# Index projection moved to the front of a hybrid RWKV/sparse-attention block, with the top-k search run beside the recurrence's preparation

## The reference, cut to what matters

```python
h = rms_norm(x, norm_mix_pre)
z = h @ w_in                      # 31 column blocks of 128
y_rwkv = rwkv7_time_mix(z_rwkv)   # r, zw, k, v, za, zg -> decays, normed keys, gates, then a scan
y_dsa  = dsa_attention(z_dsa)     # q, k, v, and index queries qi, index keys ki, index weights wi
x = x + rms_norm(concat(y_rwkv, y_dsa) @ w_out, norm_mix_post)
# then the feed-forward and the gated embedding, untouched
```

## Time and profile before

| what | value |
|---|---|
| median of 3 runs (lowest, highest) | 1964.87 us (1964.84, 1968.67) |
| the profiled execution | 1967.77 us |
| its span in the profile | 1966.3 us |
| mean granted TensorE clock | 0.947 |
| TensorE busy | 1714.4 us, 87% |
| VectorE busy | 1128.1 us, 57% |
| ScalarE busy | 771.0 us, 39% |
| GpSimd busy | 330.3 us, 17% |

### The profile page before, as it was taken

The page is one execution under the profiler, slowest core; times in us unless marked ns, Lnnn a source line. Parts: engine busy times, 40 slices in busy tenths (PEclk is TensorE's granted clock), DMA queues, the critical chain, the costliest instruction groups (busy, mean ns, idle before and its releaser), DMA issues. The chain is left out here.

```text
span 1966.3 us, 34355 instructions
## 1 busy us (share of the span) xinstructions
PE 1714.4 (87%) x14040; PEld 1388.2 (71%) x14040; DVE 1128.1 (57%) x2151; ACT 771.0 (39%) x1206; POOL 330.3 (17%) x299
## 2 busy tenths in 40 slices
PE   1899985599849995888759999999999999999996
PEld 0777663278727774777637888888888888888785
DVE  5267644779946652576643756544445654444755
ACT  4153432577535552333224433332233332322541
POOL 2232230031112210122311211000011000000422
PEclk9999997899959997999969999999999999999998
DMA  2115551122210005111035232233332333323222
GB/s 109 58 57 171 172 177 48 48 75 86 76 44 33 33 12 212 31 63 53 15 111 201 96 97 96 88 97 97 98 97 94 103 112 107 97 97 97 86 74 87
DMA packets 92182, 177.13 MB, mean 90 GB/s; under 512 B 7616, under 2 KB 51680, under 8 KB 92032
## 3 DMA queue, kind: packets, MB, share of 16 engines
q1 hardware_dynamic: 62336, 159.28, 24.4%
q10 hardware_dynamic: 29696, 15.73, 2.8%
HBM read 138.81 MB, written 36.18 MB: 89 GB/s over the span
## 5 line engine op out<-in xcount | busy, mean ns | idle before, releaser
L809 PE MATMUL acc<-h_hi,w_hi 128*128 128x512 f32 x768 | 304.8, 397 | 21.9 <-DVE w_lo L877 15.8
L810 PE MATMUL acc<-h_lo,w_hi 128*128 128x512 f32 x768 | 301.0, 392 | 0.0
L811 PE MATMUL acc<-h_hi,w_lo 128*128 128x512 f32 x768 | 300.9, 392 | 0.0
L713 ACT ACTIVATE w_hi<-w_raw 128x1024 fp32r<-128x1024 f32 x160 | 168.3, 1052 | 142.3 <-DMA w_raw<-w_ffn 142.0
L877 DVE TENSOR_TENSOR w_lo<-w_raw,w_hi 128x1024 fp32r<-128x1024 f32 x160 | 206.4, 1291 | 7.5 <-ACT w_hi L713 7.5
L809 PE MATMUL acc<-ffn_hi_lo,w_hi 128*128 128x512 f32 x512 | 200.3, 391 | 1.3 <-DVE ffn_hi_lo L925 1.3
L810 PE MATMUL acc<-ffn_hi_lo,w_hi 128*128 128x512 f32 x512 | 199.2, 389 | 0.0
L811 PE MATMUL acc<-ffn_hi_lo,w_lo 128*128 128x512 f32 x512 | 199.2, 389 | 0.0
L809 PEld LDWEIGHTS acc<-h_hi,w_hi 128*128 128x128 f32 x768 | 145.6, 190 | 55.1 <-DVE w_lo L877 16.6
L504 POOL TENSOR_TENSOR post_squares_total<-post_squares_total,post_squares 128x512 f32<-128x512 f32 x40 | 57.0, 1425 | 692.8 <-ACT post_squares L497 691.3
L810 PEld LDWEIGHTS acc<-h_lo,w_hi 128*128 128x128 f32 x768 | 145.5, 189 | 31.6 <-issue 1.7
(11 more groups left out here) (307 smaller groups left out, 3585.6 us busy)
## 6 DMA issues: line engine op xcount, KB each, us to landing
w_raw<-w_ffn SPq DMA_DIRECT2D x128, 512.0 KB, 3.4
rwkv_factors<-factors_then_masks ACTq DMA_DIRECT2D x28, 512.0 KB, 6.3
factors<-rwkv_factors SPq DMA_DIRECT2D x32, 448.0 KB, 6.8
w_in_first_raw<-w_in SPq DMA_DIRECT2D x19, 512.0 KB, 3.9
w_raw<-w_out SPq DMA_DIRECT2D x16, 512.0 KB, 3.6
w_raw<-w_gate SPq DMA_DIRECT2D x16, 512.0 KB, 3.4
w_in_raw<-w_in SPq DMA_DIRECT2D x12, 512.0 KB, 4.1
x_in<-xT SPq DMA_DIRECT2D x8, 512.0 KB, 6.7
```

What stands on the lines that cost most here:

```text
L713: act.activation(wh[:, g % RING, :], w_raw[:, g % RING, :], ACT.Copy).then_inc(rounded, 1)
L809: pe.matmul(out, w_hi, a_hi, start=first, stop=False)
L810: pe.matmul(out, w_hi, a_lo, start=False, stop=False)
L811: return pe.matmul(out, w_lo, a_hi, start=False, stop=last)
```

## The change

The norm of the input and the first five blocks become one stage, `project_index`, by halves of time: the first half of x is loaded, normed and multiplied while the second half is loaded and normed. The five blocks are the index key and weight block and the four index query blocks; their results stay on the chip. The layer norm of the index keys runs inside this stage. The mean of squares is now taken by TensorE per row block (no adding by VectorE), and all remainders of `h` are made by VectorE. `index_scores` follows at once and reads queries and keys in place. All other 26 blocks, the preparation of the recurrence and the search are one stage: 5 blocks first (low-rank, then the first pair's r, k, v), then three blocks per step for four pairs, then nine. SyncE now issues the seven stores of a pair's factors. The z blocks of r, k, v, the low-rank and the index blocks are no longer stored.

```diff
+ORDER = [KI_BLK] + [QI_BLK + b for b in range(PAIRS)] + list(range(QI_BLK)) + [b + p for b in (Q_BLK, AK_BLK, AV_BLK) for p in range(PAIRS)]
+def project_index(nc, io, common, gain, x, hi, lo, qz, kiT, wi, w):
+    units = [(0, 0), (1, 0), (0, 1), (1, 1)] + [(j, h) for j in range(2, INDEX_BLKS) for h in range(NH)]
+        def _(sp):
+            for h in range(NH):
+                for k in range(KB):
+                    sp.dma_start(x[:, k, cut[h]], io["xT"][:, k, cut[h]]).then_inc(x_loaded[h][k], 16)
+                    if h == 0 and k % 4 == 3:
+                        sp.dma_start(w.raw[:, k // 4, :], io["w_in"][ORDER[k // 4]]).then_inc(w.loaded[k // 4], 16)
+        def _(act):
+            for k in range(KB):
+                square(0, k)
+            nx[0].take_root(act)
+            w.start_rounding(act)
+            for k in range(3):
+                square(1, k)
+            for k in range(KB):
+                round_row(0, k)
+                if k + 3 < KB:
+                    square(1, k + 3)
...
+            for n in range(2, len(units)):
+                j, h = units[n]
+                copy(n)
+                if h == 1 and j + 2 < INDEX_BLKS + 2:
+                    w.round(act, j + 2, (j + 2) // 2, j % 2)
+        def _(pe):
+            for k in range(KB):
+                nx[0].sum(pe, k)
+            nx[0].spread_inverse(pe, 0)
+            for n, (j, h) in enumerate(units):
+                for k in range(KB):
+                    if n == 0:
+                        nx[1].sum(pe, k)
+                    if j == 0:
+                        pe.wait_ge(lo_ready, h * KB + k + 1)
...
+def project_and_select(nc, io, zT, hi, lo, out, rw, dec, score, mask, causal, room, va, near, vec, w):
+    BITS_AT = {WA: (0, 1, 2), G: (3, 4), FIRST_PAIR: (5, 6), FIRST_PAIR + 1: (7, 8), FIRST_PAIR + 2: (9, 10, 11)}
+    BITS_OF_PAIR = [(12, 13), (14, 15), (16, 17), (18, 19)]
+    BITS_AT.update({22: (20, 21, 22), 23: (23, 24, 25), 24: (26, 27, 28), 25: (29, 30, 31)})
+    BIAS_AT = 24
+        def _(sp):
+            for p in range(PAIRS):
...
+                sp.wait_ge(done, p + 1)
+                sp.wait_ge(vmixed, p + 1)
+                sp.wait_ge(gate_copied, p + 1)
+                for q in range(7):
+                    sp.dma_start(rw[p, :, :, q, :].rearrange("i f t -> f i t"), out[:, q, :].rearrange("f (i t) -> f i t", i=TILES)).then_inc(stored, 16)
+                load(b + 4)
+        def _(act):
+            for j in range(WA, HEAD):
+                if j > WA:
+                    round_weights(j + 1)
+                counts(BITS_AT[j])
+                copy(j)
+                if j == FIRST_PAIR + 1:
+                    act.activation(wa[0:N, :], out[0:N, 0, :], ACT.Tanh).then_inc(acted_wg, 1)
+                    act.activation(wa[N:P, :], out[N:P, 0, :], ACT.Copy).then_inc(acted_wg, 1)
+                    act.activation(sg[:, :], out[:, 1, :], ACT.Sigmoid).then_inc(acted_wg, 1)
+                    square_kk(0)
+            for p in range(PAIRS):
+                act.wait_ge(normed, p + 1)
+                act.activation(root[:, :], ps_k[:, :], ACT.Sqrt).then_inc(rooted, 1)
+                act.wait_ge(low_rank, p * 3 + 2)
+                act.activation(rate, ps_w[:, :], ACT.Sigmoid, bias=par[:, W0:W0 + 1]).then_inc(gates, 1)
+                act.activation(a, ps_a[:, :], ACT.Sigmoid, bias=par[:, A0:A0 + 1]).then_inc(gates, 1)
+                round_weights(b + 1)
+                act.wait_ge(summed, p * 2 + 2)
+...
+                copy(b)
+                round_weights(b + 2)
+                act.activation(out[:, GATE, :], ps_g[:, :], ACT.Copy).then_inc(gate_copied, 1)
+                counts(BITS_OF_PAIR[p])
+                copy(b + 1)
+                round_weights(b + 3)
+                if p + 1 < PAIRS:
+                    square_kk(p + 1)
+                copy(b + 2)
+            act.wait_ge(stored, PAIRS * STORED)
+            for j in range(FIRST_Q + 3, BLKS):
+                round_weights(j + 1)
+                counts(BITS_AT.get(j, ()))
+                copy(j)
+                if j == BIAS_AT:
+                    for h in range(HEADS):
+                        act.activation(vec[:, h, :], ps_b[:, h % 2, 0:BVEC], ACT.Copy).then_inc(bias_copied, 1)
+                if j > FIRST_V:
+                    copy_values(j - 1)
+            copy_values(BLKS - 1)
+            for j, t in enumerate(tiles):
+                act.wait_ge(selected, j + 1)
+                act.activation(mask[t][:, :], above[j % 2][:, 0:(t + 1) * P], ACT.Copy, scale=-NEG, bias=NEG).then_inc(mask_out, 1)
+        def _(pe):
+            for p in range(PAIRS):
+                pe.wait_ge(squares, p + 1)
+                by_half(ps_k, same_head[:, :], sq).then_inc(normed, 1)
+                by_half(ps_w, w2a2[0:N, :], wa[0:N, :]).then_inc(low_rank, 1)
+                pe.wait_ge(rooted, p + 1)
+                by_half(ps_a, w2a2[N:P, :], wa[N:P, :]).then_inc(low_rank, 1)
+                multiply(b)
+                by_half(ps_g, g2[:, :], sg).then_inc(low_rank, 1)
+                multiply(b + 1)
+                multiply(b + 2)
+            for j in range(FIRST_Q + 3, BLKS):
+                multiply(j)
+                if j == BIAS_AT:
+                    for h in range(HEADS):
+                        if h >= 2:
+                            pe.wait_ge(bias_copied, h - 1)
+                        pe.matmul(ps_b[:, h % 2, 0:BVEC], table[:, h, :], onehot, start=True, stop=True).then_inc(biased, 1)
+                if j > FIRST_V:
+                    turn_values(j - 1)
+            turn_values(BLKS - 1)
+        def _(dve):
+            for p in range(PAIRS):
+                dve.wait_ge(rooted, p + 1)
+                link(dve.tensor_scalar(root[:, :], root[:, :], 1e-12, None, ALU.max))
+                link(dve.reciprocal(inv[:, :], root[:, :]))
+                dve.wait_ge(gates, p * 2 + 2)
+                dve.tensor_tensor_scan(csum[:, :], keep[:, :], rate, 0.0, ALU.mult, ALU.add).then_inc(summed, 1)
...
+                dve.tensor_tensor(out[:, K_T, :], k, e_neg, ALU.mult).then_inc(done, 1)
+                find_bits(BITS_OF_PAIR[p])
+                if p + 1 < PAIRS:
+                    shift(p + 1)
...
+            for j, t in enumerate(tiles):
+...
+                if j >= 2:
+                    dve.wait_ge(mask_out, j - 1)
+                dve.scalar_tensor_tensor(above[j % 2][:, c], score[t][:, :], best[:, j:j + 1], eq[:, c], ALU.is_gt, ALU.add).then_inc(selected, 1)
```

More of the change, by code:

```diff
@@ L966, with square, sum, take_root @@
 A_T, R_T, B_T, K_T, V_T, BONUS, GATE = range(7)
-def project_and_prepare(nc, io, zT, hi, lo, out, rw, dec, w):
-    HEAD = PAIR_BLK + 3
-    COUNT = KI_BLK + 1
+class StreamedNorm(HalfNorm):
+    def square(self, act, k, src):
+        need(act, self.summed, k - self.ring + 1)
+        act.activation(self.sq[:, k % self.ring, :], src, ACT.Square).then_inc(self.squared, 1)
+    def sum(self, pe, k):
+        pe.wait_ge(self.squared, k + 1)
+        for t in range(self.QS):
+            last = pe.matmul(self.ps_mean[:, t:t + 1], self.sq[:, k % self.ring, t * P:(t + 1) * P], self.mean[:, 0:1],
+                             start=(k == 0 and t == 0), stop=(k == KB - 1 and t == self.QS - 1))
+        last.then_inc(self.summed, 1)
+    def take_root(self, act):
+        act.wait_ge(self.summed, KB)
+        act.activation(self.root[:, :], self.ps_mean[:, 0:self.QS], ACT.Sqrt, bias=self.eps[:, 0:1]).then_inc(self.rooted, 1)
@@ new lines, in project_and_select @@
+        flip, low, high, carry = [ctx.sb(n, [P, 2], U32) for n in ("order_flip", "low_half", "high_half", "carry")]
+        one = ctx.sb("one", [P, 1], F32)
+        above, equal, rank = (diff, csum), (before, wa), sg
+        table, onehot = kk[0:32, :].rearrange("b (h q) -> b h q", h=HEADS), sq[0:32, 0:BVEC]
+        sk = nc.dram_tensor("bias_skewed", (HEADS, P * (BVEC + 1)), F32, kind="Internal").ap()
+        acc = ctx.pb("z_acc", [P, 2, SEQ], F32)
+        ps_w, ps_a = [ctx.pb(n, [P, SEQ], F32) for n in ("ps_w_and_g_and_values", "ps_a_and_norm_and_bias")]
@@ L1052, in _, with counts @@
-            proj.credit_copied(act)
-            for j in range(HEAD):
-                if j >= 1:
-                    w.round(act, j + 1, (j + 1) // 2, (j + 1) % 2)
-                if j == PAIR_BLK + 1:
-                    act.wait_ge(mixed_wg, 2)
-                copy(j, place(j), j % 2)
-                if j == PAIR_BLK + 1:
+            def counts(bits):
+                for n in bits:
+                    act.wait_ge(asked, n + 1)
+                    for t in shared:
+                        j = t - FIRST
+                        act.activation(signs[t][:, :], score[t][:, :], ACT.Sign, bias=minus[:, j:j + 1], accum_out=count[:, j:j + 1]).then_inc(counted, 1)
```

939 lines of the change are left out of this document (369 added, 570 removed).

## The result

Before 1964.87 us (median of seven runs, 1959.48 to 1968.67), after **1949.58 us** (seven runs, 1943.97 to 1955.85): a ratio of 0.9931, 95% interval 0.991 to 0.9952. The change makes the kernel faster by 15.3 us, where 39 were forecast; 1949.58 lies just over the range's upper end of 1948. The profiled execution took 1948.95 us, its span is 1947.3.

The account below looks back on a forecast made before the run. TensorE was taken to gain only in three stretches without a block before 558 us. First stage and scores 149.4 plus stage three 367.8 put the last mask at 517.2, 40.8 earlier: 1926 us, range 1903 to 1948.

Parts of the forecast that it names:

- the scores: Index scores behind the first stage: unchanged work bound by VectorE, 50.4 us plus 0.6 to the next stage.
- TensorE's stand before the first root: Stage three, before the first pair's root at 69.1: TensorE stands still for 8.7 us, its low clock costing 3 more.
- blocks 26 to 30: Last blocks of stage three, forecast within blocks 25 to 30: 6 x 10.95 us with two turns of values between.
- the masks' tail: From the last block to the last mask: 5.1 + 18.2 us, so 23.3 without TensorE, as against 24 before.
- the first score matmul: End of stage one, norm and five blocks: at 98.4 us instead of 329.1, bounds 92 to 106.
- I take 15, to 37: Stage one: scaling the first half's rows takes 15 us, from about 22 to 37, slowed by averages and low clock.
- VectorE's round and TensorE's are all but equal: I take 41: Four pairs: TensorE's round 39.8 us, VectorE's 39.3, or 41 with one more GpSimd collision; so 41 a pair.
- First pair 43.3 with the low clock: First of the four pairs: 43.3 us instead of 41, as TensorE starts at the low clock.
- Cost 12.7: Bias products behind block 24: third waits for ScalarE's copy, clock falls; 12.7 us, against 5.3 if nothing waited.
- Rival B: Smoother, chance 0.20: smaller stalls at first root and bias, norm at its lower bound; 1901 us at best, likely 1910.
- rival C: Held up more, chance 0.16: clock falls in every pair, stage one at upper bound, 1943 us; two further collisions, 1957.
- rival D: Slower, chance 0.04: VectorE's round becomes the bound, every GpSimd step stretching a VectorE step by its own length; 1970 us.

Follow-up runs that it names:

- the first try of all together: Changed kernel with squares added elsewhere, masks early, bias products behind block 26, late split, one bit less beside three pairs, three bits beside block 26: 1914.16 us.

## Why the prediction was wrong

The direction and the order of the steps held; the gain of 39 us did not, and three terms of the sum were too small. As forecast came the scores, TensorE's stand before the first root (6.74 us for 8.7) with a low clock behind it, the stall at the bias, blocks 26 to 30, the length of the masks' tail and what follows (1410.9 us from last mask to end, 1409.8 before). Of the signs, the first score matmul fell outside its bounds (108.85, with 92 to 106 given), and TensorE waits for the square in two of the three rounds only. No further term for table loads was needed: those at 224.20 and 269.32 are followed by the root 0.01 us after their 1.28 us. The three terms:

- **"I take 15, to 37", and the first score matmul at 98.4** (+10.4). I took the averages as cheap work between rows (0.95 to 1.87 us for a set) and the slow pace as a matter of the first products. TensorE was in fact the bound of each row at 2.98 us, and slow until 54.6. The upper bound of 106 claimed "low clock all along" and was below what happened, because it had not added up TensorE's own row: 1.6 + 3 x 0.43 = 2.9 at the slow pace, 24 us for eight rows instead of 15. The step before was also short: the first half's eight sets ended at 21.0 instead of "near 17", and scaling began at 24.67 instead of 22. The sum is a little high against its own terms (53 + 5.5 + 32.7 + 2 is 93.2, not 93.7), which hides part of the miss. Adding the squares elsewhere takes 10.8 us back.
- **"VectorE's round and TensorE's are all but equal: I take 41"** (+7.6), and **"First pair 43.3 with the low clock"** (+1.8). The forecast had 39.8 for TensorE's round, measured 40.8 to 41.0, and 39.3 for VectorE's plus one collision of 1.75 us. VectorE had two full ones: beside A_T (3.48 instead of 1.29) or, in the first round, R_T (3.44 instead of 1.21), and k's shift (3.31 instead of 1.28), together 4.2 instead of 1.75; and, less, the clamp behind the root (1.39 to 2.15). That is 2.5 more, and the wait made `ps_k` 1.4 and 1.7 us longer: 3.9 and 4.2 by this count, 3.3 and 4.4 measured. When two engines have nearly equal rounds, what the slower one loses counts in full. Moving one split takes 3.4 and 4.4 us back. In the first round the low clock cost 4.2, not 2.3.
- **"Cost 12.7" for the bias products** (+4.4 with block 25). The stall was placed rightly (4.85 of wait and 1.28 a copy; 14.4 us in all), but I let the low clock end with it. It lasted into block 25, another 3.1, and these do not come of the stall: without it the next block was late by 2.6 and 3.0 us as well. The sum's "5.3 if nothing waited" measured 7.0 to 8.6, and the slow start behind it. Why the clock falls behind these products no run takes apart.

Rival B's condition, smaller stalls, was met by 2 us at the first root (6.74 for 8.7) and nowhere else. Of rival C's parts each held in part: stage one passed its upper bound, the clock fell behind the wait in two rounds (1.4 and 1.7 us, not 3), and one further step collided, not two. That its 1943 lies nearest to what was measured is partly luck, as those prices were not the measured ones.

The Trainium skill (GPSIMD Engine Reference, Key points) says that GpSimd contends with VectorE's instructions that have two SBUF inputs or run in a 2-port mode. For two inputs the trace agrees: A_T, both shifts and R_T are such and took 2.0 to 2.2 us longer, while three bits with a split beside them still took 11.44 us, 3.81 each (copies of blocks 22 and 23 at 412.58 and 424.02). The clamp has one input; which kind it is no run here shows. I had the page for rival D and should have counted with it in the sum which of those steps stand beside a split.

## What to carry to other kernels

When work is moved beside other work until two engines have the same round, list every step of the round that can be stretched and put the helper engine's steps where nobody waits: one wait on a semaphore brought the last mask 8.6 us forward here. Work that one engine does in order (counts, copies, masks) delays whatever stands behind it on that engine; ask of each instruction behind a slow one who needs it, and move that ahead. Before giving an engine small extra steps inside a loop, add up its own time for one turn at the slowest pace that it may have. Behind a run of small matmuls, count on a slow start of the large ones even where nobody waited: 2.4 to 3.1 us behind the bias products here.

## What the runs showed of the hardware

- A set of eight 128x1 products took 1.70 to 1.87 us at the slow pace and 0.95 at the fast one.
- Narrow products let a fast clock fall although TensorE never stood still: with wide products first the granted clock was 1.00 from 8 to 14.6 us and 0.50 from 14.8, with nothing but 128x1 products from 11.4 on. The same is seen at the bias products (32 rows, 384 columns): 1.00 from 451.8 to 456.5, 0.50 from 457 to 463.3, no wait.
- In the kernel after, with a set in front of every three products of 512 columns, the slow pace lasted until 54.6, 6 us past the last set (48.7), though TensorE was never idle from 27.6 on. With the three products alone it ended 5 us after the first of them, although TensorE had waits of 0.6 to 0.7 us after that.
- `ps_k`, four passes of 512 columns, took 3.06 to 3.65 us after waits of 1.93 to 2.78 us for its input, twelve times in seven of the runs, and 1.88 to 1.96 without a wait. So a wait of 2 us cost up to 1.7 us again. There is one exception: with the masks earlier it took 1.96 after a wait of 2.38, and the clock fell only at 361 (0.53 from 361.2 to 364.2). It also fell among the pairs' small products with no wait over 0.6 us before it (0.50 from 344.5 to 347.5 in the first try of all together).
- A VectorE step collides by what lies beside it, not by what it is for: holding GpSimd's split back by 3 us moved the same +2.0 us from one shift to the next.
- Two executions of the same instructions up to 360 us differed by 3.2 us at block 21, with a clock of 1.00 in one and 0.66 in the other from 360 to 370.
